# A fused mLSTM, convolution and expert kernel: a wait of the output projection moved from its first to its eighth product, and the block loop of TensorE unrolled

## What is computed

```python
hn = rms_norm(x, norm_mix)
proj = hn @ w_in + b_in
q, k, v, o, ig, fg, cb, cc, cx = jnp.split(proj, SPLIT_POINTS, axis=-1)
...
y_m = (jax.nn.sigmoid(o.astype(jnp.float32)) * h_m).astype(x.dtype)
y_c = short_gated_conv(cb, cc, cx, conv_w)
x = x + jnp.concatenate([y_m, y_c], axis=-1) @ w_out
hn2 = rms_norm(x, norm_ffn)
moe = hier_moe(hn2.reshape(b_sz * s_len, d), w_group, b_group, w_expert, b_expert,
               w_gate, w_up, w_down)
return x + moe.reshape(b_sz, s_len, d)
```

## Time and profile before

| | |
|---|---|
| median of 3 runs | 2148.39 us (2147.55 to 2149.42) |
| profiled execution | 2147.7 us, its span 2146.1 us |
| PE busy | 2045.3 us, 95% |
| DVE, ACT, POOL busy | 22%, 15%, 12% |
| mean granted TensorE clock | 0.979 of full speed |
| four blocks | about the first 1177 us |
| experts | about 1212 to 2093 us |

### The profile page before, as it was taken

How to read it: one execution, slowest core, us unless ns; L and a number is a source line. 1 busy time by engine, 2 the same in 40 slices (tenths; PEclk the granted TensorE clock), 3 DMA queues, 4 the chain that set the end, 5 groups by cost and what they waited for, 6 DMA issues and landing times.

```text
span 2146.1 us, 26044 instructions
## 1 busy us (share of the span) xinstructions
PE 2045.3 (95%) x10100; PEld 1405.6 (65%) x10100; DVE 471.2 (22%) x1048; ACT 329.2 (15%) x724; POOL 254.4 (12%) x272
## 2 busy tenths in 40 slices
PE   7999999999999999999999599999999999999990
PEld 3775445855547654558545588888888888888880
DVE  1034322243230443123431400000000000000003
ACT  1021110111100211102101011111111111111103
POOL 2000000000000000000000022222222222222215
PEclk9999999999999999999999699999999999999995
DMA  5312322212321123112111588888888888888868
GB/s 220 143 60 98 128 75 74 79 59 92 144 70 69 59 98 141 76 64 74 59 40 78 216 274 272 274 276 276 276 278 279 276 280 273 275 273 283 282 191 326
DMA packets 71462, 369.14 MB, mean 172 GB/s; under 512 B 8979, under 2 KB 13204, under 8 KB 39520
## 3 DMA queue, kind: packets, MB, share of 16 engines
q1 hardware_dynamic: 49584, 307.39, 39.3%
q0 software_dynamic: 16768, 43.33, 8.0%
q10 hardware_dynamic: 5040, 17.49, 2.0%
HBM read 320.67 MB, written 47.51 MB: 172 GB/s over the span
## 4 chain that ended last, share of the span: by engine, by line
PE 94%; issue 1%; DVE 1%; POOL 1%; DMA 1%; ACT 0%; POOLq 0%; ACTq 0%; DVEq 0%; SPq 0%
PE ps_proj L391 26%; PE ps_proj L561 10%; PE ps_proj L403 9%; PE ps_proj L613 7%; PE ps_proj L615 7%; PE ps_state L633 5%; PE ps_num L633 5%; PE ps_scores L615 3%; PE ps_scores L613 3%; PE ps_rows L613 3%; PE ps_rows L615 3%; PE ps_num L638 3%; PE ps_num L596 1%; PE ps_state L430 1%; POOL fss L1027 1%
## 5 line engine op out<-in xcount | busy, mean ns | idle before, releaser
L391 PE MATMUL ps_proj<-hnT,ww 128*128 128x512 f32 x1280 | 567.6, 599 | 5.3 <-issue 4.4
L391 PEld LDWEIGHTS ps_proj<-hnT,ww 128*128 128x128 f32 x1280 | 240.4, 192 | 290.0 <-issue 284.0
L561 PE MATMUL ps_proj<-wo,yT 128*128 128x512 f32 x512 | 224.5, 594 | 4.5 <-DVE yT L1301 4.5
L613 PE MATMUL ps_proj<-hnT,wo 128*128 128x160 f32 x1024 | 226.7, 303 | 0.7 <-ACT hnT L802 0.7
L403 PE MATMUL ps_proj<-ww,hnT 128*128 128x256 f32 (+1 forms) x1024 | 225.4, 381 | 0.4
L615 PE MATMUL ps_proj<-hnT,wo 128*128 128x160 f32 x1024 | 223.2, 300 | 0.0
L403 PEld LDWEIGHTS ps_proj<-ww,hnT 128*128 128x128 f32 x1024 | 193.7, 190 | 30.8 <-DVE vx L1208 2.0
L613 PEld LDWEIGHTS ps_proj<-hnT,wo 128*128 128x128 f32 x1024 | 166.5, 191 | 13.9 <-issue 13.9
L561 PEld LDWEIGHTS ps_proj<-wo,yT 128*128 128x128 f32 x512 | 95.6, 190 | 120.2 <-issue 112.4
L615 PEld LDWEIGHTS ps_proj<-hnT,wo 128*128 128x128 f32 x1024 | 167.4, 191 | 0.0
L1463 DVE TENSOR_TENSOR kT<-qT,ps_proj 128x160 f32<-128x160 f32 x64 | 17.6, 317 | 487.1 <-ACT qT L814 487.1
(11 more groups left out here) (255 smaller groups left out, 1864.2 us busy)
## 6 DMA issues: line engine op xcount, KB each, us to landing
wo<-in_w_gu SPq DMA_DIRECT2D x128, 1024.0 KB, 6.7
ww<-in_w_slots SPq DMA_DIRECT2D x52, 1024.0 KB, 4.8
og<-in_w_dn SPq DMA_DIRECT2D x32, 1024.0 KB, 5.3
vx<-in_w_dn SPq DMA_DIRECT2D x32, 1024.0 KB, 7.7
xin<-in_x SPq DMA_DIRECT2D x16, 512.0 KB, 5.6
hnT<-in_xT SPq DMA_DIRECT2D x8, 1024.0 KB, 6.9
xres<-in_x SPq DMA_DIRECT2D x16, 512.0 KB, 4.5
hn_rows<-hn ACTq DMA_DIRECT2D x16, 512.0 KB, 2.6
```

Source lines behind the costliest of these rows:

```text
L391: mm = pe.matmul(PROJ[:, n % 2, :], slot_weights(slot, k, c, P), hnT[:, k, :], start=(k == 0), stop=(k == KT - 1))
L561: mm = pe.matmul(PROJ[:, n % 2, :], yT[:, k, t * P:(t + 1) * P], wo[:, k, half * 512:(half + 1) * 512], start=(k == 0), stop=(k == KT - 1))
L613: pe.matmul(GU[m][:, 0:CAP], wo[:, kt, m * P:(m + 1) * P], xT[:, kt, :], start=(kt == 0), stop=(kt == KT - 1), skip_group_check=True)
```

## The change

PE's loop over the blocks becomes a Python loop, so that its body stands in the program four times with `b` a number, and the tests on `b` are decided when the program is built. The semaphore increment in front of the small transposes is left out. The wait in front of the output projection is for the eviction of `cb` tile MT - 2 = 2 instead of MT - 1 = 3, and the one for tile 3 now stands in front of the first result tile's last product, k = KT - 1 = 7. The other engines' programs stay as they are.

```diff
-            with pe.Fori(0, NB) as b:
+            for b in range(NB):
...
                         if kind == "q" and m in (1, 2):
-                            with pe.If(b > 0):
+                            if b > 0:
                                 if m == 1:
...
                         if kind == "k" and m in (0, 3):
-                            with pe.If(b > 0):
+                            if b > 0:
...
                 pe.wait_ge(S_("diag_ready"), b + 1)
-                own_instruction(pe)
...
-                s, k_, per = emptied(number[("cb", MT - 1)])
+                s, k_, per = emptied(number[("cb", MT - 2)])
                 pe.wait_ge(s, b * per + k_)
...
                         for k in range(KT):
+                            if t == 0 and half == 0 and k == KT - 1:
+                                s, k_, per = emptied(number[("cb", MT - 1)])
+                                pe.wait_ge(s, b * per + k_)
                             mm = pe.matmul(PROJ[:, n % 2, :], yT[:, k, t * P:(t + 1) * P],
...
                     if t == 1:
-                        with pe.If(b < NB - 1):
+                        if b < NB - 1:
                             norm_rows(b + 1)
```

## The result

The changed kernel takes 2132.68 us (median of 4 runs, 2132.53 to 2133.70), the kernel before beside it 2148.03 us (4 runs, 2147.55 to 2149.42): a ratio of 0.9928, 95% interval 0.9911 to 0.9946. The forecast was 2136.3 us with a range down to 2133.0. The direction and the three mechanisms are right.

What follows compares the result with a forecast made beforehand. TensorE (PE), busy 95% of the span, was taken as the bound. 4.3 + 4.4 + 3.4 = 12.1 us off 2147.7 gives 2135.6, plus 0.7 for the median 2136.3 us; range 2133 to 2141.

Steps and rivals of the forecast that it cites:

- the three mechanisms: Projection wait holes go (4.3 us), block-boundary jump holes go (4.4 us), clock falls behind boundaries go (3.4 us).
- What bounds the kernel: Whole span: PE is busy 95%, so whatever it saves in the blocks shortens the span by the same amount.
- Part 1: Before the output projection: moving the wait removes four holes of 1.07 us, 4.3 us gained, nothing else late.
- The `xres` add: DVE's add on the first projection tile, waiting for DMA: does not move; slack shrinks from 4.3 to 3.2 us.
- Part 2: Block boundaries: three holes of 1.46, 1.40 and 1.53 us come from the loop's jump; unrolling gains 4.4 us.
- Part 3: Start of blocks 2 and 4: without the boundary hole PE's clock does not fall, gaining 3.4 us (0 to 3.4).
- Noise: Routing step and first expert: where the clock returns may shift; no change taken, 2 us either side.
- The rivals: Clock still falls, 2139.7 (0.13); boundary holes stay, 2144.1 (0.06); moved wait blocks, 2140.6 (0.03); code fetch slower, to 2194.7 (0.03).
- The rule that the number of falls is left to chance: Clock behind block boundaries: with the hole it fell in two of three cases, so where it falls depends on chance.

Runs made afterwards that it cites:

- w_only: Kernel before with only the wait for the last conv tile moved, PE's block loop kept; 2141.13 us, 0.9971 of the kernel before.
- far_skip: Changed kernel plus a never-true test on a loaded value, jumping over 1200 products at the heads of blocks 2 to 4; 2139.80 us, 0.9967 of the kernel before.
- skip_small: Changed kernel plus a never-true test around 8 products at the heads of blocks 2 to 4; 2132.78 us.
- pair_loop: Changed kernel with PE looping over two pairs of blocks, one jump back left, and PE's semaphore increment restored; 2137.36 us.
- hole_rs2: Changed kernel plus a PE wait for POOL's last-tile scale at the heads of blocks 2 to 4; 2138.78 us, 0.9966 of the kernel before.
- u_only: Kernel before with PE's block loop unrolled and its semaphore increment left out, projection wait unmoved; 2138.72 us, 0.9959 of the kernel before.
- jump_in_o: Changed kernel with PE's block loop and semaphore increment back, the jump back placed after four o tiles; 2134.80 us.
- jump_in_q: Changed kernel with PE's block loop and semaphore increment back, the jump back behind the first q tile; 2133.86 us, 0.9940 of the kernel before.

## Why the prediction was off, point by point

- **What bounds the kernel.** Right. Nearly all of what PE saved in the blocks reached the end: 14.1 us at its last logits, 15.0 in the span.
- **Part 1.** The hole went as written, and the next thing was not late. The `xres` add stayed where it was: it ends at 247.64 + 0.69 = 248.33 after (247.90 before), and PE needs the bank at 236.94 + 2 x 6.87 = 250.7. That leaves 2.3 us of slack where 3.2 were written, and still hides it.

```profile
247.64 0.69 DVE L1377 TENSOR_TENSOR x<-ps_proj,xres 128x512 f32<-128x512 f32 x1 [8.56 <-DMA xres<-in_x]
```

- The step that failed here is its size, "By starts it is 4 x 1.07 = 4.3 us, which I take". The 1.07 us are not by starts: they run from the modelled end of the last conv pass, at 237.38, which lies 0.16 us inside the next pass when nothing is held up. By starts it is 1.71 - 0.43 = 1.28 us, 5.1 in all. Another 0.10 us is lost between the first two passes behind each hole, 0.4 in all, a term that the prediction put at nothing. `w_only` shows that both go with the hole. The row of 20.86 us was there to be read in the trace of before, beside 6.87 us for 16 passes.
- **Part 2.** The holes are the jump's, as written, and the same step failed in their size: 1.46, 1.40 and 1.53 us also run from modelled ends. By starts they are 1.63, 1.57 and 1.70 us, 4.9 in place of 4.4. That PE's code is brought anew is borne out by `far_skip` and the packets. Register work and near branches alone make no hole (`skip_small`, `pair_loop`), but behind a jump register work is 0.4 us of it. The jumps' 3.61, 3.55 and 3.68 us stood in the trace of before as well. The Trainium skill's page "Runtime: NRT & Kernel Launch" (Instruction fetch mechanics) agrees with this case: a taken branch to code that is not held forces a fetch. The 108 ns for a compare-and-branch in the Trainium skill's "Advanced Engine Details and Errata" (Control Flow Timing) would have left 4.1 us of the forecast out; for a jump to far code the trace has over thirty times as much.
- **Part 3.** Right in kind and in size: the falls went with the holes, and `hole_rs2` shows that they belong to the hole and not to the jump. By starts the two falls cost 2 x (15.53 - 13.83) = 3.4 us, as written; the undisturbed 32 passes take 13.82.
- **Noise.** The mis-sized holes are 0.8 + 0.5 us and the loss behind the projection's holes 0.4. With them the forecast would have been 2134.6, inside the range. Of the 1.9 us that are left, 0.2 lie in block 1's first tiles, 0.1 in the routing step and experts, 0.8 behind the last product with its cause open, and 0.7 are the median. The prediction carried the 0.7 us by which the median before lay above the profiled execution, and after the two are alike (2132.68 and 2132.72). So to leave the range took the mis-sized holes and, beyond them, terms that the prediction could not know; that last part is luck. The 2 us that it gave to the clock in the routing step were not needed here (53.5 us before, 53.4 after), though `u_only`, `far_skip` and `jump_in_o` took 1.2 to 1.5 us more there.
- **The rivals.** None came. The straight code is fetched without a hole, in 37 packets. The rule that the number of falls is left to chance is borne out: of 13 holes of 0.9 to 1.7 us at a boundary in five traces, 6 had a fall behind them. What PE ran ahead of the hole bears on it: the eight holes in front of the projection (before, `u_only`), with wide conv passes ahead of them, have no fall behind them. The spread of the runs points the same way, with an overlap: 1.6 to 5.7 us for kernels with boundary holes of this length, 1.2 to 2.5 us for those without.

## What to carry to other kernels

Price a hole of TensorE from start to start: the distance of the passes around it less their distance when nothing is held up. The profile's idle time and the chain count from a modelled end and give 0.16 to 0.17 us less. Then add the chance of a fall of the clock. Here a hole of 1.07 us in the chain cost 1.38, and those of 1.3 to 1.5 us cost 1.5 to 1.6, or 3.2 to 3.4 with a fall. A loop's jump is free where enough long products stand right in front of it (`jump_in_q`). Before unrolling, look at what PE does in the last 16 passes or so ahead of the jump, and rotate the loop if they are short. Where a sum's products all hang on one late operand, let the wait stand in front of the product that reads it.

## What was not expected of the hardware

- A taken jump of PE to far code takes 3.3 to 3.9 us, forward or back; one to near code 0.21 to 0.25 us, and a test that is passed through 0.07 to 0.10. PE's sequencer meets it some 16 or 17 passes ahead of the products. With short logits passes in front, 0.9 to 1.7 us show as a hole; with 16 passes of 3.5 us in all, 0.1 us or less; with 16 passes of 6.9 us, nothing.
- Behind a hole at the full clock hardly anything is lost: 0.10 us at the projection (20.70 against 20.60 us for 48 passes), 0.01 to 0.02 us at the q tiles (13.83 and 13.84 against 13.82 for 32). The larger differences that the chain shows are modelled ends.
- A hole of 0.93 us behind short logits passes was followed by TensorE's clock at 1.2 in place of 2.4 GHz (`far_skip`), as were 6 of the 13 such holes in all. Holes of 2.6 us did it three times out of three, once for twice as long. Holes of 1.0 to 1.1 us behind wide conv passes did it in none of eight cases.
